# One layer of a gated convolution and memory attention trunk: the input projection by seven block products in place of eight, and the rest in a second phase

## What is computed

```
h    = rms_norm(x, pre_norm)                        # 4096 x 1024
proj = h @ w_in_a                                   # 1024 x 5120: b, c, u, gate (1536), mq (512)
z    = c * u;  mix = b * (w0*z[t-2] + w1*z[t-1] + w2*z[t])      # causal, per column, 1024 columns
kv   = rms_norm(mem, mem_norm) @ w_mem_kv           # 256 x 1024: k and v of 4 heads of 128
o    = softmax(mq @ k.T * 128**-0.5) @ v            # 4 heads over 256 memory rows
y    = (concat(mix, o) * silu(gate)) @ w_out        # 1536 x 1024
out  = x + rms_norm(y, post_norm)
```

## Time and profile before

| | |
|---|---|
| median of three runs | 2465.9 us |
| the profiled execution, its span | 2465.2 us |
| TensorE matmul busy, share of the span | 98% |
| VectorE busy | 1263.9 us, 51% |
| ScalarE busy | 911.4 us, 37% |
| DRAM read, written | 257.45 MB, 16.78 MB |
| mean granted TensorE clock | 0.996 |

### The profile page before, as it was taken

How to read it: one execution, slowest core, us unless ns; L and a number is a source line. 1 busy time by engine, 2 the same in 40 slices (tenths; PEclk the granted TensorE clock), 3 DMA queues, 4 the chain that set the end, 5 groups by cost and what they waited for, 6 DMA issues and landing times.

```text
span 2465.2 us, 31102 instructions
## 1 busy us (share of the span) xinstructions
PE 2421.2 (98%) x10978; PEld 2010.6 (82%) x10978; DVE 1263.9 (51%) x1740; ACT 911.4 (37%) x1300; POOL 41.1 (2%) x84
## 2 busy tenths in 40 slices
PE   5999999999999999999999999999999999999997
PEld 4888888888888888888888888888888888888885
DVE  7444564445555456445555445544455445554442
ACT  4333343333433334333433334333343333433332
POOL 0000000000000000000000000000000000000000
PEclk9999999999999999999999999999999999999998
DMA  6222234222432225222252222522225222342221
GB/s 240 102 94 89 90 127 164 92 87 94 155 128 94 85 95 196 94 92 86 94 197 94 85 94 92 192 93 86 93 95 196 86 94 94 100 160 91 94 89 48
DMA packets 71852, 275.43 MB, mean 112 GB/s; under 512 B 8000, under 2 KB 8032, under 8 KB 70624
## 3 DMA queue, kind: packets, MB, share of 16 engines
q1 hardware_dynamic: 61200, 223.37, 26.8%
q0 software_dynamic: 10576, 50.88, 5.7%
HBM read 257.45 MB, written 16.78 MB: 111 GB/s over the span
## 4 chain that ended last, share of the span: by engine, by line
PE 97%; DVE 1%; DMA 0%; issue 0%; ACT 0%; SPq 0%; DVEq 0%; POOL 0%; ACTq 0%; POOLq 0%
PE banks L681 32%; PE banks L682 32%; PE banks L683 32%; PE banks L753 1%; DMA w_raw<-in_blocks 0%; DVE w_lo L452 0%; PE banks L688 0%; DVE x_in L462 0%; DVE z L457 0%; DVE h_lo L472 0%; ACT y_left L293 0%; DVE x_res L462 0%; DVE scratch L485 0%; DVE x_res L660 0%; DVE x_res L663 0%
## 5 line engine op out<-in xcount | busy, mean ns | idle before, releaser
L681 PE MATMUL banks<-h_hi,w_hi 128*128 128x512 f32 x2560 | 1001.1, 391 | 4.5 <-DVE h_lo L472 2.8
L682 PE MATMUL banks<-h_lo,w_hi 128*128 128x512 f32 x2560 | 997.8, 390 | 0.0
L683 PE MATMUL banks<-h_hi,w_lo 128*128 128x512 f32 x2560 | 997.4, 390 | 0.0
L452 DVE TENSOR_TENSOR w_lo<-w_raw,w_hi 128x1024 fp32r<-128x1024 f32 x424 | 519.0, 1224 | 377.4 <-ACT w_hi L288 366.8
L288 ACT ACTIVATE w_hi<-w_raw 128x1024 fp32r<-128x1024 f32 x413 | 435.9, 1056 | 722.3 <-PE banks L683 722.1
L681 PEld LDWEIGHTS banks<-h_hi,w_hi 128*128 128x128 f32 x2560 | 481.5, 188 | 105.3 <-issue 7.4
L683 PEld LDWEIGHTS banks<-h_hi,w_lo 128*128 128x128 f32 x2560 | 481.3, 188 | 100.4
L682 PEld LDWEIGHTS banks<-h_lo,w_hi 128*128 128x128 f32 x2560 | 481.6, 188 | 97.8
L681 PE MATMUL banks<-w_hi,g_hi 128*128 128x512 f32 x784 | 308.2, 393 | 0.9 <-DVE w_lo L452 0.9
L683 PE MATMUL banks<-w_hi,g_lo 128*128 128x512 f32 x784 | 305.1, 389 | 0.0
L682 PE MATMUL banks<-w_lo,g_hi 128*128 128x512 f32 x784 | 305.0, 389 | 0.0
(11 more groups left out here) (97 smaller groups left out, 1396.1 us busy)
## 6 DMA issues: line engine op xcount, KB each, us to landing
w_raw<-in_blocks SPq DMA_DIRECT2D x424, 512.0 KB, 3.3
x_in<-in_x_t POOLq DMA_DIRECT2D x8, 2048.0 KB, 12.2
x_res<-in_x POOLq DMA_DIRECT2D x31, 512.0 KB, 5.6
out_x<-x_res POOLq DMA_DIRECT2D x31, 512.0 KB, 4.6
x_res<-in_mem SPq DMA_DIRECT2D x1, 1024.0 KB, 4.8
post_gain<-in_post_g POOLq DMA_DIRECT2D x1, 512.0 KB, 13.2
x_in<-in_x POOLq DMA_DIRECT2D x1, 512.0 KB, 10.3
out_x<-x_in POOLq DMA_DIRECT2D x1, 512.0 KB, 2.9
```

The source lines that it names most:

```text
L452: nc.vector.tensor_tensor(w_lo[:, slot, :], w_raw[:, slot, :], w_hi[:, slot, :].bitcast(f32), ALU.subtract).then_inc(w_lo_done, 1)
L681: nc.tensor.matmul(dst, a, c, start=first, stop=False)
L682: nc.tensor.matmul(dst, a, d, start=False, stop=False)
L683: return nc.tensor.matmul(dst, b, c, start=False, stop=last)
```

## The change

The input projection is now done for two tiles of tokens together (a macro tile of 1024 tokens; four of them) and for two weight column blocks together (a pair; 20 pairs, of the kinds q, m, c, u, b, g). Each pair is a 2x2 by 2x2 block product: the weights in two halves of rows by two blocks of 128 columns, the tokens in two halves of features by two tiles. It is computed by seven products (R1, R5, R6, R3, R7, R2, R4, a scheme of Strassen's kind) of half the depth, 4 x 3 matmuls of 512 columns each, on sums and differences of the blocks. Such a product with its weights is called a unit. R1 is the first product of a pair; R6 and R7 are added to the bank of R1 and R3 to that of R5, after ScalarE has copied out what stood there (s1, p5, u2). VectorE adds the three remaining sums.

The seven token operands of a macro tile (each 4 x 512 per partition, hi and lo) lie in SBUF in one copy, `hop_hi` and `hop_lo`; `operand_hi` (ScalarE), `operand_lo` and `token_sum` (VectorE) rewrite them at each macro tile. For macro tile 0 the 140 units' weights are made on the chip (`weight_sum`, `unit_hi`, `unit_lo`), and SP stores each split unit, 512 KB, into DRAM (`w_split`). For the other three, SP loads the split units from there, six slots in all, and ScalarE and VectorE do nothing for them. The raw weights of a pair (1 MB) have a single buffer (from pair 2 on `raw_b`), loaded anew when the pair's last unit has been built. raw_b takes the place of a part of `x_in`, so that a quarter of macro tile 1's tokens is loaded at the end of macro tile 0.

The projected mq (`q_kept`), the SiLU of its gate (`m_kept`) and the gated convolution (`g_kept`) go to DRAM. The keys and values are projected inside macro tile 3, after pairs 10 to 17; the values as 128-column blocks that are transposed afterwards. In the second phase w_out is loaded once, split once and kept; the steps -9 to 63 each do a part of a head's attention, and from step 0 on a group, one half row of output for 128 tokens (12 x 3 matmuls of 512 columns). 64 groups and 32 heads in all. No loop is left: every instruction is written out. Memory addresses are laid out by hand. The core of the diff, of 2072 lines:

```
-TILE = 512
+MACROS = NT // 2
+PAIRS = 20
+PRODUCTS = 7
+ALL_PAIRS = MACROS * PAIRS
+UNITS0 = PAIRS * PRODUCTS
+KINDS = ["q", "q", "m", "m"] + ["c", "u", "b", "g"] * 4
+R1, R5, R6, R3, R7, R2, R4 = range(PRODUCTS)
+SLOTS = 6
+UNIT = 2 * HALF
+KV_BLOCKS = 2 * MH
+KV_AFTER = [3 * PAIRS + 10 + b for b in range(KV_BLOCKS)]
...
+        hop_hi = at("hop_hi", 0, [PRODUCTS, HK, T], f32r)
+        hop_lo = at("hop_lo", 56 * KB, [PRODUCTS, HK, T], f32r)
+        slots = at("slots", 112 * KB, [SLOTS, 2, HALF], f32r)
+        x_in = at("x_in", X_AT, [2, KT, T])
+        raw_b = at("raw_b", X_AT + 24 * KB, [4, HALF])
+        w_split = nc.dram_tensor("w_split", [UNITS0, P, UNIT], f32, kind="Internal").ap()
+        q_kept = nc.dram_tensor("q_kept", [MACROS, MH, 2, P, T], f32, kind="Internal").ap()
+        m_kept = nc.dram_tensor("m_kept", [MACROS, MH, 2, P, T], f32, kind="Internal").ap()
+        g_kept = nc.dram_tensor("g_kept", [MACROS, KT, 2, P, T], f32, kind="Internal").ap()
+        Y_OF = [Y11, Y12, Y12, Y22, Y11, Y21, Y21]
+        def unit_source(p, r):
+            return [raw[:, 0, :], st_w[:, 0, :], st_w[:, 1, :], st_w[:, 0, :], st_w[:, 1, :], raw[:, 1, :], raw[:, 3, :]][r]
...
+        def _(sp):
+            load_x(0, 0)
+            load_x(2, 0)
+            load_raw(0)
+            load_x(1, 0)
+            load_x(3, 0)
+            for u in range(UNITS0):
+                p, r = divmod(u, PRODUCTS)
+                slot = u % SLOTS
+                sp.wait_ge(w_lo, u + 1)
+                sp.dma_start(w_split[u], flat(slots[:, slot, :, :].bitcast(f32))).then_inc(slot_kept[slot], 16)
+                if r == R4 and p + 1 < PAIRS:
+                    if p + 1 == 2:
+                        sp.wait_ge(hop_lo_done, R3 + 1)
+                    load_raw(p + 1)
+                if (p, r) == (3, R4):
+                    sp.wait_ge(hop_lo_done, PRODUCTS)
+                    for n in range(3):
+                        load_x(n, 1)
+            load_x(3, 1)
+            for n in range(SLOTS):
+                sp.wait_ge(slot_kept[n], 16 * len(range(n, UNITS0, SLOTS)))
+            for m in range(1, MACROS):
+                for i in range(PAIRS):
+                    p = m * PAIRS + i
+                    for r in range(PRODUCTS):
+                        load_unit(UNIT_OF[p, r], i * PRODUCTS + r)
+                    if i == 3:
+                        sp.wait_ge(hop_lo_done, (m + 1) * PRODUCTS)
+                        if m + 1 < MACROS:
+                            for n in range(4):
+                                load_x(n, m + 1)
+                        else:
+                            sp.dma_start(mem_in[:], mem).then_inc(mem_dma, 16)
+                            sp.dma_start(flat(raw_kv[:]), w_kv[0]).then_inc(kv_dma, 16)
+                    if p in KV_AFTER and p != KV_AFTER[-1]:
+                        b = KV_AFTER.index(p) + 1
+                        sp.wait_ge(w_lo, UNITS0 + 2 * b)
+                        sp.dma_start(flat(raw_kv[:]), w_kv[b]).then_inc(kv_dma, 16)
...
+            for step in range(-8, 8 * NT):
+                if -8 <= step < -4:
+                    load_wo(4 + 2 * (step + 8))
+                    load_wo(5 + 2 * (step + 8))
+                if step % 2 == 0 and (step + 10) // 2 < NT * MH:
+                    load_q((step + 10) // 2)
+                if step % 2 and (step + 9) // 2 < NT * MH:
+                    load_m((step + 9) // 2)
+                if -3 <= step < 0:
+                    load_conv(step + 4)
+                if step >= 0 and step % 2 == 0 and 4 + step // 2 < NT * SUB:
+                    load_conv(4 + step // 2)
...
+        def _(act):
+            def build_hi(u, src):
+                slot = u % SLOTS
+                if u >= SLOTS:
+                    act.wait_ge(unit_done, u - SLOTS + 1)
+                    if u < UNITS0:
+                        act.wait_ge(slot_kept[slot], 16 * (u // SLOTS))
+                nc.scalar.activation(slots[:, slot, 0, :], src, ACT.Copy).then_inc(w_hi, 1)
+            def operand_hi(m, r):
+                if m:
+                    act.wait_ge(unit_done, UNIT_OF[m * PAIRS - 1, r] + 1)
+                if r == R1:
+                    act.wait_ge(normed, m * 2 * KT + HK)
+                elif r == R5:
+                    act.wait_ge(t_made, 4 * m + 1)
+                elif r == R6:
+                    act.wait_ge(t_made, 4 * m + 2)
+                elif r == R3:
+                    act.wait_ge(normed, (m + 1) * 2 * KT)
+                elif r == R7:
+                    act.wait_ge(t_made, 4 * m + 3)
+                elif r == R4:
+                    act.wait_ge(t_made, 4 * m + 4)
+                nc.scalar.activation(hop_hi[:, r, :, :], Y_OF[r], ACT.Copy).then_inc(hop_hi_done, 1)
+            def evacuate(p, r):
+                m, i = divmod(p, PAIRS)
+                kind, a = KINDS[i], bank_a[p % 2]
+                if r in (R1, R5, R6, R4):
+                    act.wait_ge(unit_done, UNIT_OF[p, r] + 1)
+                if r == R1:
+                    if p:
+                        act.wait_ge(c11_done, p)
+                    nc.scalar.activation(s1[:], a, ACT.Copy).then_inc(s1_done, 1)
+                elif r == R5:
+                    if p:
+                        act.wait_ge(c22_done, p)
+                    nc.scalar.activation(p5[:], bank_x, ACT.Copy).then_inc(p5_done, 1)
+                elif r == R6:
+                    if p:
+                        act.wait_ge(c12_done, p)
+                    nc.scalar.activation(u2[:], a, ACT.Copy).then_inc(u2_done, 1)
+                elif r == R4 and kind in "qc":
...
+            for k in range(KT):
+                square(0, k)
+            unit_hi(0)
+            act.wait_ge(consts_set, 5)
+            root(0)
+            for k in range(KT):
+                square(1, k)
+            operand_hi(0, R1)
+            unit_hi(1)
+            root(1)
+            unit_hi(2)
+            operand_hi(0, R5)
+            unit_hi(3)
+            operand_hi(0, R6)
+            unit_hi(4)
+            operand_hi(0, R3)
+            unit_hi(5)
+            for r in (R7, R2, R4):
+                operand_hi(0, r)
+            for p in range(ALL_PAIRS):
+                m, i = divmod(p, PAIRS)
+                for r in range(PRODUCTS):
+                    step = i * PRODUCTS + r
+                    evacuate(p, r)
+                    if m == 0 and step + SLOTS < UNITS0:
+                        unit_hi(step + SLOTS)
+                    if m == 0 and step >= UNITS0 - HK:
+                        square(3, step - UNITS0 + KT)
+                    if m and m + 1 < MACROS and i == PAIRS - 1:
+                        operand_hi(m + 1, r)
...
+                if p == PAIRS - 1:
+                    operand_hi(1, R1)
+                    root(3)
+                    for r in (R5, R6, R3, R7, R2, R4):
+                        operand_hi(1, r)
...
+        def _(dve):
+                if p == PAIRS - 1:
+                    add_square(3, KT - 1)
+                    operand_lo(1, R1)
+                    inverse(3)
+                    for k in range(HK):
+                        norm(3, k)
+                    token_sum(1, 0)
+                    for k in range(HK, KT):
+                        norm(3, k)
+                    operand_lo(1, R5)
+                    token_sum(1, 1)
+                    operand_lo(1, R6)
+                    token_sum(1, 2)
+                    operand_lo(1, R3)
+                    operand_lo(1, R7)
+                    operand_lo(1, R2)
+                    token_sum(1, 3)
+                    operand_lo(1, R4)
...
+            for step in range(-9, 8 * NT + 1):
+                if step % 2:
+                    n = (step + 7) // 2
+                    if 0 <= n < NT * MH:
+                        gate(n)
+                    if 0 <= n + 1 < NT * MH:
+                        soften(n + 1)
+                    if 0 <= n < NT * MH and n % MH == MH - 1:
+                        for s in range(SUB - 1):
+                            mem_split(n // MH * SUB + s)
+                    if step >= 1:
+                        mean_square(step // 2)
+                else:
+                    if 0 <= (step + 8) // 2 < NT * MH:
+                        turned((step + 8) // 2)
+                    if 0 <= (step + 10) // 2 < NT * MH:
+                        query((step + 10) // 2)
+                    if step >= 2:
+                        finish(step // 2 - 1)
+                        if step // 2 + SUB - 1 < NT * SUB:
+                            conv_split(step // 2 + SUB - 1)
+                    if step % 8 == 0 and 0 <= step < 8 * NT:
+                        mem_split(step // 8 * SUB + SUB - 1)
+                if -9 <= step < -3:
+                    wo_split(2 * (step + 9))
+                    wo_split(2 * (step + 9) + 1)
+                if -4 <= step < 0:
+                    conv_split(step + 4)
...
+        def _(pe):
+            def multiply(p, r):
```

(113 more changed lines are left out.)

1396 lines of the change are left out of this document (802 added, 594 removed).

## The result

The changed kernel takes 2487.95 us (median of four runs, 2487.27 to 2488.49), beside 2465.47 us before: 1.0091 times as long, 95% interval 1.0077 to 1.0105. Forecast were 2456 us and "faster" with the better chance; it is slower.

What follows compares the result with a forecast made beforehand. The prediction took the kernel to be bound by TensorE's count of matmuls. Its terms, 2191 + 70 + 36 + 43.5 + 25 + 4 + 71 + 15, summed to 2455.5, taken as 2456 us; range 2420 to 2505.

Steps and rivals of the forecast that it cites:

- TensorE's work, 2191 us: Whole kernel: 9216 matmuls of 512 columns, 576 of 256, 264 transposes and six token sums together take 2191 us.
- Start, 70: Before R6 of the first pair: TensorE stands still 70 us, including 3 for low clock; range 55 to 80.
- Macro tile 0, 36: Building units in macro tile 0: 36 us of standstill from raw-weight reloads, late VectorE adds, and the norm and inverse.
- First crossing, 43.5: Macro tile 0 to 1: operands prepared only then, R6 held by s1; 43.5 us of standstill, 38 to 50.
- Later crossings, 25: Macro tiles 1 to 2 and 2 to 3: late add, late s1 and clock fall, 12.5 us each, 25 together.
- Loading, 4: Loading split units keeps up; up to 2 us could show at the four x loads: 4 us in all, 0 to 15.
- Phase two, 71 and nothing: Second phase: bare attention chains at low clock before group 0 cost 71 us, 50 to 85; from then on 0.
- rival (b): Start, crossings and phase two's first steps: TensorE's bursts keep the full clock, giving 2426 us; chance 0.19.
- End, 15: After the last matmul: 5.5 us of final row work, and 9.6 from last issue to end; 15 us.
- (a): Macro tile 0: raw loads land later behind SP's store, so ScalarE waits and u2 is late; 2480 to 2540, chance 0.24.
- (c): Start, crossings and phase two: the fills are hidden as in the kernel before, giving 2231 us; chance 0.02.
- (d): All units: pace falls through waits every 12 matmuls or late code fetch, 28 us, giving 2484; chance 0.05.

Runs made afterwards that it cites:

- Experiment 7: Changed kernel with ScalarE copying out R1, R5 and R6 between its operand copies at the start and first crossing, not after all seven: 2478.53 us.
- experiment 3: Changed kernel with GpSimd's stores behind pair 3 and g pairs in macro tile 0 waiting for R3 of the next pair: 2477.93 us.
- experiment 5: Changed kernel with a second raw-weight buffer, so from pair 2 on loads, cut into quarters, go a whole pair ahead: 2420.06 us.
- experiment 9: Changed kernel with added matmuls, results unread, ahead of TensorE's waits in phase two's steps -9 to -1: 2486.05 us.
- q first alone: Changed kernel with SP loading the next q ahead of the two w_out rows in phase two's steps -8 to -5: 2486.61 us.
- e8_all: Changed kernel with raw loads in quarters, moved builds, earlier copies and token sums, filler matmuls, and q loaded ahead of w_out: 2432.61 us.
- experiment 2: Changed kernel with SP issuing the raw load ahead of the store of the unit just built, not behind it: 2479.44 us.
- e1_quarters: Changed kernel with each pair's raw weights loaded in four quarters, each once its own last reader is done: 2452.57 us.
- e9_two_buffers: Changed kernel with separate raw-weight buffers for even and odd pairs, loads in quarters, a pair ahead from pair 2 on: 2420.06 us.

## Why the prediction was wrong

Step by step; a term measured is the stretch in the trace after less its work at the full pace.

- **TensorE's work, 2191 us: right.** 44 matmuls of macro tile 1 lie between 800.09 and 810.07, 0.2268 each as before, and the page counts 9216 of 512 columns. (2486 less all standstill and low clock listed here, 294, is 2192, but most of those terms were found by taking the forecast work off.)
- **Start, 70: right (71).** R6 started at 74.4 (forecast 72.7), released by ScalarE's s1, not by its operand. Experiment 7 moved the copies.
- **Macro tile 0, 36: wrong, it was 69.** This is the step that failed, and alone it makes the miss of 30 us in the span. Of the 36, 25 were R7's waits (15 x 0.8 + 4 x 3.3) and 11 VectorE's late adds and the norm. (1) The load's round trip was too short: R7's waits were 43.2 us in 19 stops. In seven u and g pairs they were 0.9 to 1.8, near the forecast, and in b pairs 2.4 to 4.1 (3.3 forecast), where the convolutions delay the load's issue. But in the other eight pairs they were 2.0 to 4.3 where 0.8 was forecast. Seven of these stand behind a q, m or g pair, where GpSimd stores 1 MB 1.9 to 4.1 us before SP issues the load (6.6 to 9.0 us from issue to use); for four of them experiment 3 shows that this store is the cause. (2) The stops bring low clock. I had priced a fall behind each of the big fills and none here, a term put at nothing without a reason. The granted clock was 0.96 over 446 us, as it had been 0.57 over five in the kernel before: 0.04 x 446 is 18 us. (3) VectorE's adds hold TensorE for 3.5 us in place of 11, and without a late load for none (experiment 5). The remaining 4 us are my estimate for matmul rows that overlap: a stop costs 0.16 us more than its idle time, 24 times. With the loads a pair ahead, 68 of the 69 us are gone.
- **First crossing, 43.5: right (43.7).** 46.3 us from the last unit to R6. 2048-element splits took 2.29 us, as interpolated.
- **Later crossings, 25: about right (20).** Stops of 3.6 and 2.8 us where 3.5 and 5.9 were forecast.
- **Loading, 4: right (5).** 1.0 and 2.0 us behind the x loads.
- **Phase two, 71 and nothing: right (72 and nothing), but for one reason that is not.** The first score comes 14.7 us after the last unit (12.6 forecast) and group 0 another 72.1 later (71.6), and the clock is low, as forecast; yet experiment 9 shows that the low clock is not what makes it long, so that rival (b)'s 15 us were not to be had by the clock alone. That the size came out is in part luck: the forecast put 15 us of it down to the low clock. Fills alone take 1.4 us from the stretch, q first alone 3.9, both (e8_all) 10.
- **End, 15: right (13.6).**
- **The rivals.** (a) is the one that came: slower, ScalarE's wait for the raw load, 19 times. Its place and mechanism were as written. Its cause was not: it named the store ahead on SP's queue, which is worth 8.5 us (experiment 2); the other queue's store is worth 10 at the four loads tested (experiment 3), and most of the rest is the round trip itself: in an ordinary pair the data came 8.2 us after R1's product (2.25 to the issue, 5.9 to landing), and R7 allows 6.9. It had 0.24, and with the margin between "faster" and "slower" at 15 us of a 260 us sum of fills, it deserved more. (b) did not come: the granted clock was 0.79, 0.62 and 0.59 in the fills. Nor did (c), nor (d), which the pace of 0.2268 rules out.

What stays open: how much each link costs in the first steps of phase two. q's load holds the scores of heads 1 and 2; the rest of the chain on ScalarE and VectorE was not varied, nor were the fills' own microseconds separated from what the clock gave. And why the loads behind the stores of pairs 0 to 2 are late was not tested apart.

## What to carry to other kernels

A single buffer that is refilled when its last reader is done costs a full round trip per refill, and it is paid by whatever stands behind the first reader in that engine's stream; compare round trip and slack before comparing busy times (VectorE at 252 of 378 us cost nothing once the loads came a pair ahead). Short stops of TensorE have to be priced twice, once for the stop and once for the clock: here 47 us of stops came with 18 of clock. And when one wait is removed and another engine shows as releaser, look for what that engine itself waited before believing that it is full.

## What the runs showed of the hardware

- A 1 MB load on SP's queue took 5.5 to 6.0 us from issue to use. Issued 1.9 to 4.1 us behind a 1 MB store into DRAM by GpSimd it took 6.6 to 9.0 (seven loads). For four of them, at 7.1 to 9.0, the store was moved away, and they took 5.5 to 5.8 (experiment 3). SP's own issue took between 0.82 and 1.27 us there in place of 0.43.
- SP's stores of 512 KB into DRAM landed in 2.7 us on the median and its loads of the same size in 3.6 (kernel after; they belong to different macro tiles). Over the other kernels the stores took 2.6 to 4.5 and the loads 3.3 to 4.1, so neither is faster as a rule.
- A load of 256 KB took 4.7 us on the median (e1_quarters) where one of 1 MB took 5.9, and 5.5 where four were issued together (e9_two_buffers): cutting a load in four wins mostly by the earlier start.
- Stops of 0.9 to 4.3 us, one in some 23 us, are enough for stretches at the lower clock (0.96 on the mean of 446 us); the same kernel without them has 1.00. It fell in or right behind eight of the 19 stops, each of 2.0 us or more (as after the one shown above: 0.50 from 360.7 to 363.9), and at none of the seven of 0.9 to 1.8. Four of 2.1 to 2.6 us passed without a fall, so the length of the stop alone does not decide.
